# Hybrid decoder layer on 8 cores: attention's deferred VectorE work paced by an estimate, one GpSimd product, a deeper start of the merge and a last tile by banks

## The reference, cut to what matters

```python
# BATCH 4, SEQ 2048, D_MODEL 2048, 8 heads, two softmax maps per head of dimension 64, value dimension 128
proj = rms_norm(x) @ w_in            # -> q, k, v, z_a, u_glu, z_c, ga, gc
p = softmax(mask(q @ k^T / 8))       # causal, two maps per head
o = (p[0] - lam * p[1]) @ v          # per head
o = rms_norm(o) * (1 - lam_init) * silu(z_a)
y_attn = o @ w_o_attn
u = silu(layer_norm(causal_conv31(glu(u_glu)))) * silu(z_c)
y_conv = u @ w_pw2 + b_pw2
m = sigmoid(ga) * y_attn + sigmoid(gc) * y_conv
x = x + rms_norm(m @ w_out)
```

## Time and profile before

| | us |
|---|---|
| three timed runs | 1183.41, 1187.24, 1218.34 (median 1187.24) |
| profiled execution | 1181.25 |
| its span (core 6, the slowest) | 1179.7 |
| even cores 0, 2, 4, 6 | 1177.5, 1176.5, 1179.7, 1179.7 |
| odd cores 1, 3, 5, 7 | 1169.8, 1171.2, 1171.2, 1168.9 |

### The profile page before, as it was taken

How to read it: one execution, slowest core, us unless ns; L and a number is a source line. 1 busy time by engine, 2 the same in 40 slices (tenths; PEclk the granted TensorE clock), 3 DMA queues, 4 the chain that set the end, 5 groups by cost and what they waited for, 6 DMA issues and landing times.

```text
span 1179.7 us, 21808 instructions; the slowest of 8 cores (1168.9 to 1179.7 us)
## 1 busy us (share of the span) xinstructions
PE 1096.0 (93%) x8042; PEld 674.0 (57%) x8042; DVE 551.1 (47%) x1290; ACT 323.7 (27%) x500; POOL 102.1 (9%) x196
## 2 busy tenths in 40 slices
PE   2699999999999998899888999999999999999995
PEld 1355556886666774577444566666666666654442
DVE  5573444426556136766677633333333333315333
ACT  3442223432101165566444311111111111102111
POOL 1111010011101100000000001101101010000000
PEclk9899999999999998899899999999999999999998
DMA  8929767554665632322142305337266183064442
GB/s 251 220 46 174 143 114 150 106 86 81 139 135 113 139 57 57 57 49 51 37 73 37 55 18 108 55 53 114 46 128 110 34 144 57 16 179 161 158 160 95
DMA packets 49792, 118.11 MB, mean 100 GB/s; under 512 B 5520, under 2 KB 11920, under 8 KB 46352
## 3 DMA queue, kind: packets, MB, share of 16 engines
q0 software_dynamic: 27648, 62.93, 32.8%
q1 hardware_dynamic: 21744, 53.53, 14.9%
q10 hardware_dynamic: 288, 0.18, 0.0%
HBM read 162.94 MB, written 16.58 MB: 152 GB/s over the span
## 4 chain that ended last, share of the span: by engine, by line
PE 81%; DVE 9%; issue 3%; DMA 3%; ACT 3%; DVEq 0%; SPq 0%; ACTq 0%
PE ps L1291 21%; PE ps L816 11%; PE ps L1343 11%; PE ps L770 10%; PE ps L649 9%; PE ps L1301 5%; PE ps L1295 5%; PE ps L693 3%; PE ps L1021 2%; PE ps L922 2%; DMA r<-usc 2%; PE ps L899 2%; DVE zoz L970 1%; DVE r L1028 1%; DVE r L958 1%
## 5 line engine op out<-in xcount | busy, mean ns | idle before, releaser
L1291 PE MATMUL ps<-hTo,wring 128*128 128x384 bf16 x1536 | 257.5, 326 | 0.0
L1291 PEld LDWEIGHTS ps<-hTo,wring 128*128 128x128 bf16 x1536 | 150.3, 98 | 99.2
L164 POOL DMA_DIRECT2D wring<-wp x176 | 93.4, 549 | 835.9 <-PE ps L1291 242.0
L649 PE MATMUL ps<-hTo,wring 128*128 128x384 bf16 x768 | 130.9, 332 | 9.9 <-ACT hTo L545 4.2
L770 PE MATMUL ps<-wring,hTo 128*128 128x256 bf16 x1152 | 135.6, 273 | 1.2 <-PE ps L899 1.2
L1308 ACT ACTIVATE zoz<-zoz 128x384 f32<-128x384 f32 x96 | 50.0, 522 | 315.3 <-DVE zoz L1306 315.3
L816 PE MATMUL ps<-hTo,wring 128*128 128x384 bf16 x768 | 125.0, 326 | 0.0
L770 PEld LDWEIGHTS ps<-wring,hTo 128*128 128x128 bf16 x1152 | 108.6, 98 | 21.2 <-issue 8.3
L1306 DVE TENSOR_TENSOR zoz<-ps,R 128x384 f32<-128x384 f32 x96 | 53.5, 558 | 128.0 <-PE ps L1291 127.8
L649 PEld LDWEIGHTS ps<-hTo,wring 128*128 128x128 bf16 x768 | 75.6, 100 | 63.1 <-issue 16.5
L905 ACT ACTIVATE r<-ps 128x1024 bf16<-128x1024 f32 (+2 forms) x104 | 92.8, 905 | 47.6 <-PE ps L899 44.2
(11 more groups left out here) (114 smaller groups left out, 1016.1 us busy)
## 6 DMA issues: line engine op xcount, KB each, us to landing
wring<-wp POOLq DMA_DIRECT2D x176, 256.0 KB, 7.1
r<-usc SPq DMA_DIRECT2D x32, 295.2 KB, 8.2
hTo<-xr SPq DMA_DIRECT2D x9, 1024.0 KB, 6.8
out<-hTo SPq DMA_DIRECT2D x18, 512.0 KB, 3.3
r<-xf SPq DMA_DIRECT2D x11, 768.0 KB, 9.2
r<-wop POOLq DMA_DIRECT2D x4, 1024.0 KB, 13.8
zoz<-wop POOLq DMA_DIRECT2D x4, 1024.0 KB, 14.9
r<-wout POOLq DMA_DIRECT2D x4, 1024.0 KB, 20.5
```

Of the source, the lines that this page charges most:

```text
L164: eng.dma_start(out=it[1][0], in_=it[1][1]).then_inc(self.dsem[it[2]], 16)
L649: t.op('pe', lambda e, dc=dc, x=x: e.matmul(bank(2 * par + x, n), lhsT=w[:, dc, 128 * x:128 * x + 128], rhs=hTo[:, dc, c:c + n], start=(dc ...
L1291: t.op('pe', lambda e, dc=dc, k=k, w=w, o=o, cs=cs, c0=c0, n=n: e.matmul(o[k], lhsT=w[:, dc, cs], rhs=hTo[:, dc, HALO + c0:HALO + c0 + n], ...
```

## The change

1. `late` with its fixed rate becomes two queues. `urgent` holds the operations of a slot, `lazy` the roots and scalings. The recorder keeps an estimate of the time that PE and VectorE have been given (`now`, `spent`). `pump` puts a deferred operation on VectorE's list only while VectorE's estimate is at most 1 us ahead of PE's, once per step and once per filler piece.
2. The root is taken for two heads at once (18 columns), after the odd head. For this there are 4 output buffers `osb` and 6 of `accs` (2 and 4 before).
3. A mask is issued one step later than its exponential.
4. In a z_c piece, tanh is issued one step later and the last VectorE product another step later. The product with u moves to GpSimd, so VectorE has two operations a piece in place of three.
5. The filler is divided anew over the quarters (`H.fill`). Two weight panels change places so that they are still used in order.
6. The merge begins with the heads (gates and convolution branch) of two iterations before the last transposes, which use banks 2 and 6.
7. The last output tile is squared, multiplied and written bank by bank, in four pieces of 512 columns from the SP and ACT queues. Each piece is multiplied by the norm weight before the root is known.

```diff
-            self.rate = 6
+            self.fill = ((('v', 1), ('z', 0, 1)), (('v', 2), ('z', 2)), (('z', 3), ('v', 3), ('z', 4)), (('z', 5, 6, 7),))
...
-            self.rate = 4
+            self.fill = ((('v', 1), ('z', 0)), (('z', 1), ('v', 2)), (('z', 2, 3), ('v', 3)), (('z', 4, 5, 6, 7),))
...
+    def spent(e, us):
+        now[e] = (max(now['dve'], now['pe']) if e == 'dve' else now['pe']) + us
...
+    def pump():
+        while now['dve'] <= now['pe'] + 1.0:
+            for q in (urgent, lazy):
+                if q and q[0][1] <= now['pe']:
+                    run_first(q)
+                    break
+            else:
+                return
...
+    def run_zlate(flush=False):
+        while zlate:
+            zlate.pop(0)()
+            if not flush:
+                return
...
         for n in range(len(pairs)):
+            run_masks()
             if n + 2 < len(pairs):
                 emit_qk(n + 2)
-            run_late(H.rate)
+            run_zlate()
+            pump()
             yield 1.0
             emit_pv(n)
...
                 t.op('dve', lambda e: e.tensor_tensor(out=zv, in0=bank(b, n), in1=rv, op=ALU.mult), reads=[('ps', b)] + rn, writes=[('zt', p)])
-                t.op('act', lambda e: e.activation(out=sv, in_=zv, func=AF.Tanh, scale=0.5), reads=[('zt', p)], writes=['zs'])
-                t.op('dve', lambda e: e.scalar_tensor_tensor(out=zv, in0=sv, scalar=1.0, in1=zv, op0=ALU.add, op1=ALU.mult),
-                     reads=[('zt', p), 'zs'], writes=[('zt', p)])
-                t.op('dve', lambda e: e.tensor_tensor(out=uv, in0=uv, in1=zv, op=ALU.mult),
-                     reads=[('zt', p), ('u2T', cc, g)], writes=[('u2T', cc, g)])
+                spent('dve', 0.6)
+                t.op('pool', lambda e: e.tensor_tensor(out=zw[p][:, 0:n], in0=uv, in1=zv, op=ALU.mult),
+                     reads=[('zt', p), ('u2T', cc, g)], writes=[('zw', p)])
+                def tanh():
+                    t.op('act', lambda e: e.activation(out=sv, in_=zv, func=AF.Tanh, scale=0.5), reads=[('zt', p)], writes=['zs'])
+                def prods():
+                    t.op('dve', lambda e: e.scalar_tensor_tensor(out=uv, in0=sv, scalar=1.0, in1=zw[p][:, 0:n], op0=ALU.add, op1=ALU.mult),
+                         reads=[('zw', p), 'zs'], writes=[('u2T', cc, g)])
+                zlate.extend((tanh, prods))
...
+                if it == 0:
+                    merge_head(0, 0, 0, 0)
+                    merge_head(1, 0, 0, 1)
+                    f_begin()
+                elif it > 1:
+                    merge_head(it, pi, ci, tg)
+                merge_tail(it, pi, ci, tg)
...
+        for k in range(4):
+            g_mm(i, k)
+            g_square(i, b0 + k, k)
+            if k == 3:
+                t.op('dve', lambda e: e.tensor_reduce(out=ssq2[:, i:i + 1], in_=ssq4, axis=AX.X, op=ALU.add),
+                     reads=[('ssq4', x) for x in range(4)] + ['small'], writes=[('ssq2', i)])
+            t.op('dve', lambda e, k=k: e.tensor_tensor(out=ov(k), in0=bank(b0 + k), in1=wvs[:, 512 * k:512 * k + 512], op=ALU.mult),
+                 reads=[('ps', b0 + k), 'wvs', ('ssq4', k)], writes=[('ol', k)])
+        g_root(i, [])
+        for k in range(4):
+            t.op('dve', lambda e, k=k: e.scalar_tensor_tensor(
+                out=ov(k), in0=ov(k), scalar=rstd2[:, i:i + 1], in1=xr[par][:, 512 * k:512 * k + 512], op0=ALU.mult, op1=ALU.add),
+                reads=[('xr', par), ('ol', k), ('rstd2', i)], writes=[('ol', k)])
+            t.dma(('sp', 'act')[k % 2], io["out"][i * 128:(i + 1) * 128, 512 * k:512 * k + 512], ov(k), reads=[('ol', k)], key=('outl', k))
```

More of the change, by code:

```diff
@@ L369, in program @@
     rcol = small[:, 16:32]
-    nt_v, nt_i, nt_a, nt_b = (small[:, 64 + 16 * k:80 + 16 * k] for k in range(4))
+    nt_v, nt_i, nt_a, nt_b = (nt[:, 18 * k:18 * k + 18] for k in range(4))
     lamt = small[:, 128:136]
@@ L435, in program @@
     zs = m.f32(FM)
+    zw = [m.f32(FM) for k in range(2)]
+    if not NX:
+        assert m.at <= 2 * (16 * NO + 16384)
     m = Bump(r1)
@@ new lines, in finalize, with scaled @@
+            late(urgent, fk, 0.46, lambda sub=sub, oi=oi, on=on, i=i: t.op('dve', lambda e: e.scalar_tensor_tensor(
+                out=t0s[:, sub, :], in0=oi, scalar=1.0, in1=oi, op0=ALU.mult, op1=ALU.mult, accum_out=ssqh[:, h, i:i + 1]),
+                reads=[on, 'small'], writes=['t0s', ('ssqh', h, i)]))
+        if si == NS - 1 and h % 2:
+            hs = (h - 1, h)
+            for f in rsqrt_ops(rstdp[:, 9 * (h - 1):9 * (h - 1) + 18], ssqp[:, 9 * (h - 1):9 * (h - 1) + 18], 18, 1.0 / 128, 1e-5,
+                               [('ssqh', x, i) for x in hs for i in range(NT)], [('rstdh', x) for x in hs]):
+                late(lazy, h - 1, 0.27, f)
+            def scaled(x, i):
+                v = zoz[:, i, 128 * x:128 * x + 128]
+                t.op('dve', lambda e: e.scalar_tensor_tensor(out=v, in0=osb[x % 4][:, i, :], scalar=rstdh[:, x, i:i + 1], in1=v,
@@ L971, in scaled @@
                                                              op0=ALU.mult, op1=ALU.mult),
-                     reads=[('osb', h % 2, i), ('rstdh', h), ('oz', i, h)], writes=[('oz', i, h)])
+                     reads=[('osb', x % 4, i), ('rstdh', x), ('oz', i, x)], writes=[('oz', i, x)])
                 if i == NT - 1:
-                    oz_done.add(h)
-            f += [lambda i=i: scaled(i) for i in range(NT)]
-            late.extend((fk + 1, x) for x in f)
+                    oz_done.add(x)
@@ L978, in att_stream @@
+            for x in hs:
+                for i in range(NT):
+                    late(lazy, h - 1, 0.28, lambda x=x, i=i: scaled(x, i))
     def att_stream():
@@ L1245, in program @@
         raise AssertionError
-    run_late(len(late))
+    run_zlate(True)
+    while urgent:
+        run_first(urgent)
+    while lazy:
+        run_first(lazy)
     def f_load(n):
@@ L1275, in f_begin, with merge_head @@
         wop_load(1)
-    it = 0
-    for pi in range(8):
+    def merge_head(it, pi, ci, tg):
         sa, sc = (2 * pi) % 4, (2 * pi + 1) % 4
@@ new lines, in merge_head @@
+        cs = slice(128 * ci, 128 * ci + 128)
+        c0, n = H.fg[tg]
+        b0 = 4 * (it % 2)
+        for k, w, slot in ((0, wga, sa), (1, wgc, sc)):
+            for dc in range(16):
+                t.op('pe', lambda e, dc=dc, k=k, w=w: e.matmul(
+                    bank(b0 + k, n), lhsT=w[:, dc, cs], rhs=hTo[:, dc, HALO + c0:HALO + c0 + n], start=(dc == 0), stop=(dc == 15)),
+                    reads=[('W', slot, dc // 4)] + own_res, writes=[('ps', b0 + k)], sig=(dc == 15))
+        for fc in range(8):
+            t.op('pe', lambda e, fc=fc: e.matmul(
+                bank(b0 + 3, n), lhsT=wopb[pi % 2][:, 1, fc, cs], rhs=uT[:, fc, 32 + c0:32 + c0 + n], start=(fc == 0), stop=(fc == 7)),
+                reads=[('wop', pi % 2)] + [('u2T', c, tg) for c in range(8)], writes=[('ps', b0 + 3)], sig=(fc == 7))
@@ L1356, in g_out @@
              reads=pres + ['small'], writes=['junkG', ('ssq2', i)])
[L1357 to L1359 removed]
+        g_root(i, pres)
         for hh in range(2):
```

205 lines of the change are left out of this document (109 added, 96 removed).

## The result

The changed kernel takes 1170.64 us in the median of four runs (1169.39 to 1173.5), against 1185.78 for the kernel before beside it. The ratio is 0.9892 with a 95% interval of 0.9875 to 0.9908. It is faster by 1.1%. That is less than the 2% that the chances went by, so "within 2%" came true. The time lies 2.6 us over the predicted 1168. The profiled execution took 1171.47 us.

The account below looks back on a forecast made before the run. Bound: PE, held up in the attention by VectorE's order, in half 1 only in its last part. Half 1: 1171.2 - 12 - 1.5 + 10.8 - 3 = 1165.5, profiled 1167, median forecast 1168 us; range 1152 to 1183.

Parts of the forecast that it names:

- within 2%: Whole kernel: the new time differs from the old by less than 2%, here 24 us; chance 0.75.
- The sum: Whole kernel: half 1 ends at 1165.5 us, half 0 at 1159.1, so the odd cores become the slower ones.
- Entry: Merge start: PE waits for late weights and runs partly at lower clock, +10.8 us in half 1, +14.9 in half 0.
- the cover: Merge start: second head and stall hide VectorE's longer flush before the transposes; without that some 3 us more.
- Two heads: Merge start: two heads before the transposes hide 1.5 us of waiting for VectorE's flush, -1.5 us in both halves.
- Attention: Attention stage: pacing and later masks and tanh let PE set the pace, -31 us in half 0, -12 in half 1.
- near 330: Sign to look for: half 1's attention near 330 us, with clocks of 0.97 or more.
- four chunks in place of five: Half 1's attention: its last quarter gets four z_c chunks, not five, named in support of the 12 us gain.
- The product: z_c pieces in the attention: one product on GpSimd takes 0.9 us, between 0.56 and 1.23.
- GpSimd holds VectorE back: Rival, attention: each GpSimd product delays VectorE's two-input operations, 21.6 us in half 0; 1182 us, or 1171 for half; chance 0.12.
- The last tile: Kernel end: working by banks takes 5.2 us from last matmul to VectorE's last operation, was 7.9; -3 us in all.
- The first rival: Merge start: weights arrive in time, only 2 us of the entry felt; 1158 us, or 1155; chance 0.24.

Follow-up runs that it names:

- e1: The changed kernel with the merge's first weight loads issued ahead of the last quarter's products on GpSimd's list; 1155.42 us, ratio 0.9757 to the kernel before.
- e5: Against e1, the old start of the merge: one head before the transposes, which use four banks; 1159.63 us.
- e9: The changed kernel with loads ahead and the product on VectorE, but tanh and the closing product issued at once; 1161.76 us.
- e8: Against e1, the old division of the filler and the old panel order; 1149.85 us in a single execution.
- e2: The changed kernel with the z_c product back on VectorE, loads where the change has them; 1157.1 us, ratio 0.9771 to the kernel before.

## Why the prediction was right, and where it wasn't

**The sum.** The exchange of the slower half and the cause named for it, the loads behind the products, were right. That the time came within 2.6 us of 1168 is in part luck. With measured terms, core 3: 1171.2, attention -14.2, entry and merge +18.5, tail -3.2, and an attention that started 2.5 us earlier: 1169.8, where the prediction has 1165.5. Core 2: 1176.5 - 26.3 + 18.3 - 3.2 + 1.4 = 1166.7, where it has 1159.1 from core 6. In half 1 the entry with the two heads was 9.2 us too low on core 3 (7 us in the mean of the four odd cores), the gain of the attention was also put too low (2.2 us on core 3, 5 in the mean), and the attention's start, 2.5 us earlier there, is not in the sum at all. These errors stood against one another. The last step was a slip: from 1167 for the profiled execution, "2 to 6 us above" makes 1169 to 1173, and I wrote 1168. In the event the median lay 0.8 us under the profiled execution.

**Entry: the wait right, its consequences mis-sized.** 8.4 and 12.7 us of waits on cores 3 and 2 against 8.3 and 12.4; over all cores they were 8.2 to 11.0 and 10.5 to 12.7. I gave the lower clock 2.5 us "between 0 and 5". It took 7.5 on core 3; on core 2 the first head ended 23.5 us after the last value product, less 12.7 of waits and 6.5 of work, so 4.3. This term is the step that failed: it was 4.2 to 7.5 us on the eight cores, above the stated bound on six of them by my reading. On core 3 nearly the whole first head ran at 0.50; on core 2 12 of the gate matmuls and the 8 of the branch did, so "part of what follows" was right there and still twice too cheap. That wop landed at 24.8 us and not 17.5 hardly enlarged the waits; as I read it, PE needed the time for the panels at half its clock. The entry was worth 14 to 18.5 us in half 1 and 17 to 18.4 in half 0; I had 9.3 and 13.4 with the cover.

**Two heads.** "-1.5 in both halves" failed. With the loads ahead (e1) entry and merge take 290.5 and 375.0 to 376.6 us, before 290.1 and 375.8: nothing gained, since the transposes on two banks bring gaps of 0.74 and 1.2 us of their own. The "some 3 us" without the cover became 3 to 6 (e5).

**Attention.** In half 0, 31 predicted, 26.3 to 30.8 core by core; the forecast of 216 us was 2 to 3 short. In half 1, 12 predicted, 14 to 20 measured. The "near 330" was counted from 425.4, 14 us ahead of the first score; from there on it means 316, and 313 came. I held lateness to be rarer there, but tanh at once costs half 1 5 to 6.5 us (e9), almost as much as half 0. The credit for "four chunks in place of five" was wrong: the old five are 2 us better in half 1 (e8). The reason given for half 0, "all that PE waited for was order", fits what came: the waits went, and the clock rose with them from 0.93 to 0.99. But which change of order did it is shown for less than half of the gain only.

**What of the bundle did it.** In half 0 the runs attribute some 11 to 13 of about 28 us: tanh later 7.4, mask later 2.4, the estimate 1.4 to 3. They are summed as if they were independent, which only one pair was tried for. The other 15 us or so stay open. Left of the change are the roots of two heads at once (9 us less busy time for VectorE), 6 `accs` buffers in place of 4 (an operation is issued at the latest when its slot's buffer comes up again, so with 4 sooner), and the order that takes a slot's operations ahead of roots and scalings; none was tried alone. In half 1, some 7 of 14 to 20 are attributed.

**The product.** 0.9 us predicted, 0.917 measured at 384 columns (1.04 at 448). The rival "GpSimd holds VectorE back" had the lock right and came true in its first step: some 13 us of the 21.6 were there, and they cancelled what the move saved VectorE. It failed on its last step: PE's attention is the same in e1 and e2, for VectorE has 70 us to spare in it.

**The last tile.** 5.2 us from the last matmul to VectorE's last operation, measured 4.5 on core 2, against 7.9:

```profile
1156.09 0.60 ACT L1426 ACTIVATE uT<-ps 128x512 bf16<-128x512 f32 x1 [2.77 <-PE ps L1417]
1156.88 0.16 DVE L1465 TENSOR_REDUCE small<-small 128x1 f32<-128x4 f32 x1 [2.76 <-ACT uT L1426]
1157.59 0.15 DVE L1432 RECIPROCAL small<-small 128x1 f32<-128x1 f32 x1
1157.85 2.74 DVE L1471 SCALAR_TENSOR_TENSOR hTo<-hTo,small 128x512 f32<-128x512 f32 x4
```

The tail fell by 3.0 to 3.5 us on every core, 3 predicted.

**The first rival** (the weights arrive in time, 1158 or 1155) is not what the change does, but what e1 made of it: 1155.4.

## What to carry to other kernels

An engine's list that carries weight loads should get no computation with a late input in front of them: look at every queue that a moved operation is put on, and issue the loads first. When the busiest engine is starved for a few microseconds, price the work between and after the stalls at the lower clock as well as the stalls themselves. Count what the moved operation does to the engine that it leaves: here the lock took back all the time that VectorE had saved in half 0. And try each part of a bundle alone: here the estimate was worth a microsecond, the new division less than nothing, and a step's delay for tanh a quarter of the gain in half 0.
